# Three FP32R transformer blocks on one core: byte places of the split activations and of the slots of the split weights

## What is computed

```python
def first_block(x, ...):                       # two layers
    for i in range(2):
        h = rmsnorm(x, mix_norm[i])
        x = x + (pool_mixer(h, ...) if i == 0 else chunk_attention(h, ...))   # attention: 16 heads, banded
        h = rmsnorm(x, ffn_norm[i])
        x = x + conv_ffn(h, ...)               # (silu(conv3(h Wgate)) * (h Wval)) Wout, 2816 wide
    return x

def second_block(x, ...):                      # one layer
    proj = rmsnorm_2(x, norm_attn) @ w_in      # rq rk rv rg sq sk sv ga gb, 6656 wide
    x = x + (sigmoid(ga) * (retention @ w_branch_ret) + sigmoid(gb) * (stick_breaking @ w_branch_sb)) @ w_out
    hn = rmsnorm_2(x, norm_ffn)
    return x + peer(hn, ...)                   # 16 of 16384 experts a head: gates, u table, v table
```

## Time and profile before

| | us |
|---|---|
| median of 3 runs | 1532.61 |
| lowest and highest | 1531.12, 1533.7 |
| the profiled execution | 1531.16 |
| its span in the trace | 1529.4 |

### The profile page before, as it was taken

One profiled execution on the slowest core, in us unless ns is written; L12 is line 12 of the kernel. 1 busy time (PEld: TensorE's weight loads), 2 busy tenths in 40 slices (PEclk: granted clock), 3 DMA queues, 4 the chain that ended last, 5 costly groups with the idle time before them and its releaser, 6 DMA issues.

```text
span 1529.4 us, 26335 instructions
## 1 busy us (share of the span) xinstructions
PE 1499.0 (98%) x10162; PEld 1378.1 (90%) x10162; DVE 1106.1 (72%) x2153; ACT 765.5 (50%) x1562; POOL 334.6 (22%) x240
## 2 busy tenths in 40 slices
PE   6999999999999999999999999999999899999998
PEld 6999997799999977899999999999999877777777
DVE  6766678767666765766768895566666688898987
ACT  7554565555555546544344123443443366666665
POOL 1111113202111121101016011222222134344340
PEclk9999999999999999999999999999999999999999
DMA  5666666445666563444554587888888889999996
GB/s 188 187 190 194 192 193 208 124 139 179 189 187 191 170 215 121 140 140 134 179 158 138 158 283 241 295 290 295 293 286 301 274 284 334 344 334 348 335 351 215
DMA packets 95851, 344.68 MB, mean 225 GB/s; under 512 B 10664, under 2 KB 11952, under 8 KB 95728
## 3 DMA queue, kind: packets, MB, share of 16 engines
q1 hardware_dynamic: 77296, 275.89, 55.6%
q0 software_dynamic: 18432, 67.12, 12.3%
HBM read 341.92 MB, written 1.05 MB: 224 GB/s over the span
## 4 chain that ended last, share of the span: by engine, by line
PE 85%; DVE 6%; DMA 3%; ACT 3%; issue 2%; POOL 1%; DVEq 0%; SPq 0%; ACTq 0%; POOLq 0%
PE ps L1004 84%; DMA RAW<-wall 3%; DVE WL L436 2%; ACT WH L608 1%; DVE YS L1523 1%; DVE HL L1523 1%; POOL FS L522 1%; DVE XT L1520 0%; ACT HH L626 0%; PE ps L1160 0%; DVE SS L1523 0%; POOL SM L489 0%; DVE MX L1714 0%; PE ps L1179 0%; DMA XT<-xt 0%
## 5 line engine op out<-in xcount | busy, mean ns | idle before, releaser
L436 DVE TENSOR_TENSOR WL<-RAW,WH 128x1024 fp32r<-128x1024 f32 x361 | 443.0, 1227 | 180.0 <-ACT WH L608 159.4
L608 ACT ACTIVATE WH<-RAW 128x1024 fp32r<-128x1024 f32 x354 | 372.7, 1055 | 245.5 <-PE ps L1004 233.4
L1004 PE MATMUL ps<-XT,RAW 128*128 128x192 f32 x2048 | 343.9, 327 | 0.5 <-DMA RAW<-wall 0.5
L1004 PEld LDWEIGHTS ps<-XT,RAW 128*128 128x128 f32 x2048 | 331.5, 190 | 0.7 <-ACT BIG L901 0.7
L1004 PE MATMUL ps<-HH,WH 128*128 128x256 f32 x976 | 276.9, 284 | 0.4 <-DVE WL L436 0.4
L1004 PE MATMUL ps<-WH,GG 128*128 128x512 f32 x768 | 267.2, 400 | 5.7 <-DVE GG L1520 5.4
L1004 PE MATMUL ps<-HL,WH 128*128 128x256 f32 x976 | 272.7, 279 | 0.0
L1004 PE MATMUL ps<-HH,WL 128*128 128x256 f32 x976 | 272.4, 279 | 0.0
L1004 PE MATMUL ps<-WL,GG 128*128 128x512 f32 x512 | 202.7, 396 | 0.0
L1004 PEld LDWEIGHTS ps<-WH,GG 128*128 128x128 f32 x768 | 145.4, 189 | 47.0 <-DVE GG L1520 12.6
L1004 PEld LDWEIGHTS ps<-HH,WH 128*128 128x128 f32 x976 | 183.5, 188 | 3.1 <-issue 2.5
(11 more groups left out here) (271 smaller groups left out, 2448.5 us busy)
## 6 DMA issues: line engine op xcount, KB each, us to landing
RAW<-wall SPq DMA_DIRECT2D x510, 512.0 KB, 4.3
B<-rel SPq DMA_DIRECT2D x4, 768.0 KB, 6.1
DEC<-con SPq DMA_DIRECT2D x4, 384.0 KB, 4.4
XT<-xt SPq DMA_DIRECT2D x4, 256.0 KB, 5.4
UB<-utab,IDXU POOLq DMA_INDIRECT x64, 7.5
VB<-wall,IDXV POOLq DMA_INDIRECT x64, 8.1
WIN<-con SPq DMA_DIRECT2D x1, 768.0 KB, 8.4
out<-XT SPq DMA_DIRECT2D x2, 256.0 KB, 2.5
```

The lines of the kernel that those rows point to most:

```text
L436: ins = eng.tensor_tensor(wl, RAW[:, b % NRAW, :], wh.bitcast(F), ALU.subtract)
L608: act.activation(halves(b)[0], RAW[:, b % NRAW, :], ACT.Copy).then_inc(s_hi, 1)
L1004: return pe.matmul(o, l, r, start=start, stop=stop, skip_group_check=True)
```

## The change

It moves operands within a partition and leaves every instruction, its shape, its order and its waits as they are.

- WH and WL get 8 unused columns (32 bytes) behind each slot: slot 0 stays at 0 modulo 128, slot 1 is at 32, slot 2 at 64.
- HH and HL get 32 columns more, and the halves of phase r begin `HALF_AT[r]` columns into them. HH and HL themselves still begin at 32 modulo 128, so the halves of x lie at 64 in phases 0 and 1, 32 in phase 2, 96 in phase 3, 0 in phase 4 and 32 in phase 5.
- Everything behind them moves up by 256 or 512 bytes and so keeps its place modulo 128.

Places modulo 128 bytes, before and after:

| | before | after |
|---|---|---|
| slots 0, 1, 2 of WH and WL | 0, 0, 0 | 0, 32, 64 |
| HH and HL in phases 0 to 5 | 32 in all | 64, 64, 32, 96, 0, 32 |
| EH, FH, AH, SBH, RTH, MH and their low halves | 64 | 64 |
| GG, RAW, XT | 0 | 0 |

```diff
+HALF_AT = [8, 8, 0, 16, 24, 0]
...
-        WH, WL = sb("WH", [128, NSPLIT, BLK], R), sb("WL", [128, NSPLIT, BLK], R)
+        WH, WL = (sb(n, [128, NSPLIT * (BLK + 8) + 8], R)[:, 0:NSPLIT * (BLK + 8)].rearrange(
+            "p (s c) -> p s c", s=NSPLIT)[:, :, 0:BLK] for n in ("WH", "WL"))
...
-        HH, HL = sb("HH", [128, KD, T], R, early), sb("HL", [128, KD, T], R, early)
+        HX = [sb(n, [128, KD * T + 32], R, early) for n in ("HH", "HL")]
+
+        def x_halves(r):
+
+            return [t[:, HALF_AT[r]:HALF_AT[r] + KD * T].rearrange("p (k t) -> p k t", t=T) for t in HX]
+
+        def entry_of(b):
+
+            return max(r for r in range(6) if ENTRY[r] <= b)
...
-            def block(b, o, hi=HH, lo=HL, per_k=None, done_k=None):
+            def block(b, o, hi=None, lo=None, per_k=None, done_k=None):
+                if hi is None:
+                    hi, lo = x_halves(entry_of(b))
...
-                        ins = mm3(bank[two[t_]][:, :], HH[:, k, c128(t_)], HL[:, k, c128(t_)], wh[:, c], wl[:, c],
+                        hi, lo = x_halves(entry_of(b))
+                        ins = mm3(bank[two[t_]][:, :], hi[:, k, c128(t_)], lo[:, k, c128(t_)], wh[:, c], wl[:, c],
```

More of the change, by code:

```diff
@@ L625, in enter @@
                         act.wait_ge(s_x, 8 * r - 8 + m + 1)
-                    act.activation(HH[:, m, :], XT[:, m, :], ACT.Identity, scale=par_col(GAIN[r], m)).then_inc(s_hh, 1)
+                    act.activation(x_halves(r)[0][:, m, :], XT[:, m, :], ACT.Identity, scale=par_col(GAIN[r], m)).then_inc(s_hh, 1)
                     if r not in (2, 4) and m in (1, 3, 5):
@@ L1104, in tensor_program @@
                             c = slice(512 * g2 + 256 * k, 512 * g2 + 256 * k + 256)
-                            ins = mm3(bank[t_ + 2 * half][:, o:o + 256], HH[:, 2 * g + k, c128(t_)],
-                                      HL[:, 2 * g + k, c128(t_)], WH[:, half, c], WL[:, half, c],
+                            hi, lo = x_halves(0)
+                            ins = mm3(bank[t_ + 2 * half][:, o:o + 256], hi[:, 2 * g + k, c128(t_)],
+                                      lo[:, 2 * g + k, c128(t_)], WH[:, half, c], WL[:, half, c],
                                       g2 == 0 and k == 0, k == 1)
@@ L1561, in x_low @@
                     dve.wait_ge(s_hh, 8 * r + m + 1)
-                    stt(HL[:, m, :], XT[:, m, :], par_col(GAIN[r], m), HH[:, m, :].bitcast(F), ALU.mult,
+                    stt(x_halves(r)[1][:, m, :], XT[:, m, :], par_col(GAIN[r], m), x_halves(r)[0][:, m, :].bitcast(F), ALU.mult,
                         ALU.subtract).then_inc(s_hl, 1)
```

## The result

The changed kernel takes 1535.23 us, the median of 18 runs (1534.07 to 1539.34); the kernel before took 1531.84 in 18 runs beside it. The ratio is 1.0025, interval 1.0018 to 1.0032. So it is slower, by 3.4 us in the medians and by about 3.8 us (0.25%) by the ratio; the low end of the interval is 0.18%. The forecast was 3.8 us faster, so the time moved the other way, although it lies inside the range. The profiled execution took 1534.44 us, its span is 1532.6.

A forecast was written before the change was run, and what follows sets the result against it. TensorE, busy 1499.0 of 1529.4 us, was taken as the bound, so its savings come off the end one for one. The terms summed to -3.8 us against the median 1532.6, giving 1528.8 us, range 1522 to 1537.

The forecast's parts named there:

- Term 1: Val blocks of both feed-forward phases, 40 ring blocks: d from 32 to 64, 2.80 to 2.73 us each, -2.8 us.
- Term 2: Out0 blocks of phase 1, 20 blocks: d from 64 to 0, 2.80 us each, +1.4 us; bounds 0 and +3.0.
- d: Byte place of the streamed operand less that of the stationary one, modulo 128; taken to price each matmul.
- both rows, out0 and rbr: Profile rows for blocks with d = 64: out0 2.73 us (113.8 ns a matmul), rbr 2.83 us (117.9).
- the 2.88 us of rows 7: Two early blocks with HH at 32 and slots at 0, 120.0 ns a matmul; upper bound for out0.
- In phase 3 out1 has slot 0 and doesn't change: Out blocks of the second feed-forward phase: places kept, so no change, staying at 2.73 us.
- Terms 3, 4, 5: Blocks rg, ga, gb: -0.4 us; the 28 blocks with AH, SBH, RTH, MH: -0.6; pq ring blocks: +0.2.
- Term 6: 512-column w and second-mixer natural blocks: about 560 matmuls come to d = 64, -2.8 ns each, -1.6 us.
- the slower one: Rival: streams starting at the same place (d = 0) collide, out0 above all; +6.3 us, 1538.9 us; chance 0.16.
- The first rival: Place decides nothing; how one block hands over to the next sets a rhythm; all terms 0, 1532.6 us; chance 0.28.
- The cover: ScalarE and VectorE costed at nothing: 77 and 51 us idle of 162 in a feed-forward phase; TensorE hardly waits for them.

The follow-up runs named there:

- probe_rounds: Computation left out: rounds of val, gate and out blocks alone on TensorE, 20 placements; before's placement took 117.1, 116.7, 113.5 ns, the change's 117.6, 116.9, 118.8.
- x_only: The changed kernel without the slots' 8 unused columns, so only the halves of x move by phase; ratio to the kernel before 1.004 (1.0026 to 1.0054).
- slots_only: The changed kernel without the places by phase (HALF_AT all 0), slots still 32 bytes apart; ratio to the kernel before 1.0025 (1.0013 to 1.0036).
- wl_pad: pads_only with HH and HL at their old sizes, so WL alone moves 128 bytes against WH; ratio 1.0024 (1.0015 to 1.0033).
- even_256: The whole change, with pads that keep WL and HL an even multiple of 128 from WH and HH; ratio to the kernel before 1.0018 (1.0009 to 1.0027).
- pads_only: The changed kernel with only its unused bytes, every place modulo 128 as before, WL and HL pushed 128 modulo 256; ratio to before 0.9988 (0.9979 to 0.9997).
- phase3_moved: pads_only with HH and HL at 96 modulo 128 in the second feed-forward layer; ratio 1.0 (0.9991 to 1.0009).
- gg_only: The kernel before with one tensor 128 bytes longer, so GG moves from 0 to 128 modulo 256; 1530.85 us, ratio 0.9982 (0.9968 to 0.9996).
- probe_chains: Computation left out: chains of 48 256-column matmuls at chosen places, each after an idle gap, nothing else running; 113.3 to 120.0 ns with low halves even.
- places_256: The kernel before with HH, HL, FH 192 past the slots modulo 256, GG and attention's HH level with them; 1516.13 us, ratio 0.9882; profiled again 1520.86, 0.992.

## Why the prediction was wrong

**The step that failed is the rule by which terms 1 and 2 were priced: that d modulo 128 fixes a block's time, so that a d can take its price from the row of the stage it stands in.** What the runs show in its place: a block's time goes by places modulo 256, those of the low halves included, and even these leave a choice. At 64 and at 192 there are two rhythms, 113.3 to 113.8 and 117.7 to 117.8. The prediction had both rows, out0 and rbr, said that they contradict each other, and took the lower "since out0 stands in the same phase".

- *Term 1*, val blocks to d = 64: forecast -2.8, bound +1.2, measured +0.7. They took 117.8, the rbr value. The phase was no guide. Here modulo 256 says no more than modulo 128 (d is 64 by both). 113.3 was within reach of these high places in probe_rounds with the low halves even; whether the padding's shift of WL and HL lost it or what ran ahead did isn't shown.
- *Term 2*, out0 to d = 0: forecast +1.4, measured +2.5. I priced d = 0 by half a 512-column matmul, 116.6. The chains show 120.0 for 256 streamed columns at one place, and out0 has 119.2. The 512-column w blocks say nothing of it: in them the places are 128 apart modulo 256 (GG 0, slots 128), which modulo 128 looks like 0. The upper bound, the 2.88 us of rows 7, was nearly reached (2.86).
- *"In phase 3 out1 has slot 0 and doesn't change"*: measured +2.3, the largest miss. x_only and slots_only each have it (117.5 and 118.5), wl_pad and even_256 in part (116.4 and 115.6), pads_only and phase3_moved hardly (113.9 and 114.4). gg_only, which moves neither slots nor halves, has 113.5 in one profile and 117.9 in two, so both are allowed at the places of before. In two profiles each, before has the one and the change the other. What picks it stays open.
- *Terms 3, 4, 5*: -0.4, -0.6, +0.2 forecast; +0.5, +0.3, +0.2 measured. Small, two of three with the wrong sign.
- *Term 6*, 512 columns: -1.6 forecast, about -2.4 measured, of it -1.6 in the w blocks. Right in size, wrong in reason. I put it on d = 64 (slot 2 in the w blocks); slot 0, which didn't move, gained most (231.0), and pads_only has more than all of it (-2.4 ns) with no d changed. It comes from WL and HL an odd 128 away from WH and HH, which I took to be free since all behind the longer tensors "keeps its place modulo 128".

Of the rivals, the slower one came nearest. It said that d = 0 collides and d = 64 goes the way of rbr, and that it decides once out0 takes over 2.85 us and term 1 is lost: out0 takes 2.86 and term 1 is lost. Its +6.3 missed out1 and the 512-column gain. The first rival, that a stream falls into a rhythm and keeps it, had hold of the other half: places allow rhythms, history picks one. I had set the two against each other; each holds in part. That the measured time lies inside the range is owed to the width that the rivals gave it, not to the terms.

The cover held. Waits, VectorE, ScalarE and the direct blocks cost nothing, as forecast. That the granted clock is full "in every slice" read too much into a row of 9s: 6.8 us at the first w block run at the lower level, which cost 2.1 us before and 2.6 after and so hardly touches the sum.

In probe_chains nothing else runs, and places alone move a matmul from 113.3 to 120.0 ns. The Trainium skill, SBUF — State Buffer, "Who interferes with whom", gives TensorE a read port for the streamed operand and another for the weights, and speaks of contention between engines. The section says nothing of byte places; that none matters was my conclusion from it, and the chains contradict that conclusion. The chains and blocks here never came under 113.3 ns for 256 columns and 226.7 for 512. The Trainium skill, TensorE: Matmul & The Clock Gate, "Wait — 56ns, not 53.3ns?", has columns by 2.4 GHz and about 2.5 ns, which makes 109.2 and 215.8 ns as estimates; no block of float32r matmuls here reached them.

## What to carry to other kernels

Where TensorE is the bound and its matmuls read float32r at full rate, lay out streamed and stationary operands by their places modulo 256, low halves included; here the best were 192 apart for 256-column blocks and level for 512, and 1% of the kernel hung on it. Price such a move only from a chain with the same full placement, and even then as one of two values, since a placement can have two rhythms. A padding that looks neutral also moves everything behind it, and a row from another stage may be another rhythm. Profile the same code twice before giving 2 us in 1530 to an edit.

## What the runs showed of the hardware

- Equal matmuls, at a full granted clock and with nothing else running, take 113.3 to 120.0 ns by the places of their operands (256 float32r columns, low halves even; up to 121.5 with them odd), and 226.7 to 234.4 for 512. With the low halves even, the distance modulo 256 gives the time of most chains; these blocks of the kernels fit it without having been used for it: val0 on EH, 224 apart, 118.3 in before (table 118.3); the same blocks in places_256, 0 apart, 119.7 (table 120.0); wo and rbr, 64 apart, 117.8 in most slots (table 117.8). Not all do: gate0 and gate1 of even_256, both 160 apart, took 120.2 and 118.6 (table 117.2), and out1 there, 64 apart, 115.6.
- Such a chain keeps its pattern over many blocks, and identical code can take another in its next execution, worth 2.4 us of 1529 in gg_only. The kernels' runs, 1527.91 to 1537.27 us for gg_only alone, spread by more than that; that all of it is rhythms wasn't shown. The stretch at the lower clock is another source: it lasts 3.4 us in four of the fifteen profiles of whole kernels and 6.8 in the others, and costs 1.6 to 2.9 us.
- TensorE's granted clock fell to half, its lower level, within a wait of 4.6 us in the kernel before, and was full again after 6.8 us, in 4.5 of which matmuls ran: 512 columns took 0.43 us there, 0.23 behind it.
- In the w blocks a faster TensorE gives back part of the gain: 4.4 ns less in each of 1270 matmuls is 5.6 us, and the stretch from w 1 on became 0.3, 3.4 and 3.0 us shorter than before's in three profiles of gg_only, measured against its first profile; in the second profile of before the same stretch was 1.2 us longer than in the first, so the gain is known to about that. The 16 DMA engines are 95% busy there in this row of the windows of the kernel before:

```profile
1375.00:1450.00 75.00, 74.92 (x319) 59.13 (x318) 67.30 (x84) 46.49 (x94) 31.92 (x18) 1.00 0.95 341
```

What makes these rhythms inside the chip, a bank, a port or a buffer, no run here tells.
